# Values of the sampled cross attention: cached rows as weights instead of probabilities as weights

## The reference

```python
def cross_attn(h, mk, mv, wq, wo):
    B, T = h.shape[:2]
    q = (h @ wq).reshape(B, T, CA_HEADS, CA_HD)
    s = jnp.einsum('bthd,bmhd->bhtm', q, mk).astype(jnp.float32) * CA_HD ** -0.5
    p = jax.nn.softmax(s, axis=-1)
    o = jnp.einsum('bhtm,bmhd->bthd', p.astype(mv.dtype), mv).reshape(B, T, CA_HEADS * CA_HD)
    return o @ wo
```

## Time and profile before

| | us |
|---|---|
| median of three runs | 1419.38 |
| the three runs | 1419.38, 1414.24, 1420.62 |
| the profiled execution, its own time | 1415.52 |
| its span, first to last instruction | 1413.7 |
| TensorE busy | 1278.7 (90% of the span) |
| TensorE's weight loads | 1132.2 (80%) |
| VectorE, ScalarE, POOL busy | 538.9, 437.6, 393.7 |

### The profile page before, as it was taken

The page is one execution under the profiler, slowest core; times in us unless marked ns, Lnnn a source line. Parts: engine busy times, 40 slices in busy tenths (PEclk is TensorE's granted clock), DMA queues, the critical chain, the costliest instruction groups (busy, mean ns, idle before and its releaser), DMA issues.

```text
span 1413.7 us, 20837 instructions
## 1 busy us (share of the span) xinstructions
PE 1278.7 (90%) x9132; PEld 1132.2 (80%) x9132; DVE 538.9 (38%) x697; ACT 437.6 (31%) x731; POOL 393.7 (28%) x245
## 2 busy tenths in 40 slices
PE   6996998999889799898968999797999999999995
PEld 5995455777548799787867998496999999999994
DVE  4122143654121325565250034125666666630003
ACT  5224544554331312332132333212222222221111
POOL 1141102000121326122545420032443344433440
PEclk9998998999899899778988999899999999999998
DMA  6332312000341424201444333411122222222211
GB/s 193 121 93 75 112 45 99 22 1 1 105 165 33 124 86 164 75 8 45 154 159 149 120 120 148 180 60 60 60 90 90 90 90 90 90 83 83 83 53 63
DMA packets 91209, 130.14 MB, mean 92 GB/s; under 512 B 6472, under 2 KB 78560, under 8 KB 88816
## 3 DMA queue, kind: packets, MB, share of 16 engines
q1 hardware_dynamic: 83104, 101.61, 22.0%
q0 software_dynamic: 8016, 27.21, 5.7%
HBM read 120.38 MB, written 12.59 MB: 94 GB/s over the span
## 4 chain that ended last, share of the span: by engine, by line
PE 81%; DVE 8%; ACT 5%; DMA 2%; issue 2%; POOL 2%; SPq 0%; DVEq 0%; ACTq 0%; POOLq 0%
PE ring L658 42%; PE ring L632 5%; PE hold L766 5%; PE hold L863 3%; PE ring L1103 2%; PE ring L991 2%; PE ring L834 2%; PE hold L951 2%; POOL weight_lo L563 2%; PE ring L609 2%; PE hold L921 2%; PE ring L642 1%; PE ring L845 1%; PE ring L1185 1%; ACT arena L1437 1%
## 5 line engine op out<-in xcount | busy, mean ns | idle before, releaser
L563 POOL TENSOR_TENSOR weight_lo<-w_ring,weight_hi 128x1024 fp32r<-128x1024 f32 (+1 forms) x124 | 301.0, 2429 | 570.6 <-ACT weight_hi L1324 562.9
L658 PE MATMUL ring<-operand_hi,weight_hi 128*128 128x272 f32 (+1 forms) x1296 | 274.4, 293 | 28.4 <-POOL weight_lo L563 10.3
L658 PE MATMUL ring<-operand_lo,weight_hi 128*128 128x272 f32 (+1 forms) x1296 | 271.6, 291 | 0.0
L658 PE MATMUL ring<-operand_hi,weight_lo 128*128 128x272 f32 (+1 forms) x1296 | 271.4, 291 | 0.0
L1324 ACT ACTIVATE weight_hi<-w_ring 128x1024 fp32r<-128x1024 f32 (+1 forms) x135 | 139.9, 1038 | 369.0 <-PE ring L658 306.2
L658 PEld LDWEIGHTS ring<-operand_hi,weight_hi 128*128 128x128 f32 (+1 forms) x1296 | 206.4, 191 | 33.6 <-issue 23.8
L658 PEld LDWEIGHTS ring<-operand_hi,weight_lo 128*128 128x128 f32 (+1 forms) x1296 | 206.1, 190 | 0.4
L658 PEld LDWEIGHTS ring<-operand_lo,weight_hi 128*128 128x128 f32 (+1 forms) x1296 | 205.8, 190 | 0.4
L1304 ACT ACTIVATE arena<-ring 128x1024 f32<-128x1024 f32 (+10 forms) x113 | 81.2, 725 | 180.3 <-PE ring L658 59.9
L766 PE MATMUL hold<-arena,w_ring 128*128 128x504 f32 (+1 forms) x192 | 81.9, 536 | 12.5 <-ACT arena L1437 7.4
L2233 DVE TENSOR_TENSOR x_res<-x_res,ring 128x544 f32<-128x544 f32 x24 | 17.3, 721 | 186.9 <-PE ring L658 186.6
(11 more groups left out here) (360 smaller groups left out, 1975.6 us busy)
## 6 DMA issues: line engine op xcount, KB each, us to landing
w_ring<-in_w_in SPq DMA_DIRECT2D x13, 1024.0 KB, 5.3
w_ring<-in_ffn_w_gate SPq DMA_DIRECT2D x11, 1024.0 KB
w_ring<-in_ffn_w_up SPq DMA_DIRECT2D x11, 1024.0 KB, 5.3
w_ring<-in_ffn_w_down SPq DMA_DIRECT2D x8, 1024.0 KB, 5.1
arena<-in_cache_mem_k SPq DMA_DIRECT2D x6, 1024.0 KB, 6.9
arena<-in_cache_mem_v SPq DMA_DIRECT2D x6, 1024.0 KB, 10.3
w_ring<-in_w_out SPq DMA_DIRECT2D x4, 1024.0 KB, 5.3
w_ring<-in_ca_wk SPq DMA_DIRECT2D x4, 1024.0 KB, 6.5
```

The source lines that it names most:

```text
L563: self.ops.tensor_tensor(half_of(WL, self.x, kk, cols), w, half_of(WH, self.x, kk, cols).bitcast(F32), ALU.subtract).then_inc(sem("weights ...
L658: last = mm(ps[0:cols, hf * 512:hf * 512 + HALF], half_of((WH, WL)[pw], x, KT, cols)[:, i, :], (xh, xl)[px][:, k, hf * HALF:(hf + 1) * HAL ...
```

## The change

The roles of the operands are swapped. A tile of value rows, 128 tokens x 128 features, becomes the weights, and the four probability columns of one head of one sample are streamed. The result is feature-major, 128 features x 4 tokens, and is written where it belongs in a `ring` item of 128 x 256 (8 feature tiles x 32 sample columns), so that one copy by ScalarE takes it to `MX`. The hold item `cO`, the copy to `crow` and the eight transposes are gone. The samples are taken one by one in the order of the loads, and each signals `cross_values_used` (or `psum_full` for the last), so that SP waits for two signals instead of one. The other sample's columns of `yPT` are not read any more; POOL's memset of them is gone, and with it its wait, and ScalarE waits for the end of the key output (`mem_k_out`) itself, since `yPT` lies over the buffer which that output reads.

```diff
--- before.py
+++ after.py
@@ -286,7 +286,7 @@
     hold = [("h",) + x for x in CGROUPS] + [("o", i, g) for i in range(QT) for g in range(NG)]
     for rd in range(2):
         hold += [("Ss", rd), ("Sw", rd), ("PV", rd)]
-    hold += [("As",)] + [("dSs", h) for h in range(HH)] + [("cS",), ("cO",)]
+    hold += [("As",)] + [("dSs", h) for h in range(HH)] + [("cS",)]
     raws = [("c", kv, n) for kv, g4 in CGROUPS for n in group_tiles(kv, g4)]
     for rd in range(2):
         raws += [(k, rd, b) for k in ("sk", "wk", "sv", "wv") for b in range(4)]
@@ -439,7 +439,6 @@
         KX = take("ca", 2048).rearrange("p (s n) -> p s n", s=2)
         norm_rows = nc.alloc_sbuf_tensor_at("norm_rows", [P, 1024], F32, offset=base["rstd"])[:, :]
         KT4 = [KX[:, 0, :], KX[:, 1, :], mst_all[:, 768:1792], norm_rows]
-        crow = QC.rearrange("p k t -> p (k t)")[:, 0:DM]
 
         def rounded(name, at, n):
 
@@ -1218,25 +1217,17 @@
             cross_probs_t(3)
             cross_weigh(3)
             evac(pe, ("csPT",))
-            open_hold(("cO",))
-
-            for pair in ((0, 2), (4, 6), (1, 3), (5, 7)):
-                for b in pair:
-                    _, s, c = cross_in("v", b)
-                    pe.wait_ge(s, c)
-                for hf in range(2):
+            ps = open_item(("csO",))
+            for b in (0, 2, 4, 6, 1, 3, 5, 7):
+                raw, s, c = cross_in("v", b)
+                pe.wait_ge(s, c)
+                for d in range(KT):
+                    q = 16 * (b % 2) + DS * (d // 2)
+                    at = d * NSMP + DS * b
                     for j in range(2):
-                        for b in pair:
-                            q = 32 * (b // 2)
-                            last = mm(HOLD[q:q + 32, hf * 512:(hf + 1) * 512], yPT[:, j, b, :],
-                                      cross_in("v", b)[0][:, j, hf * 512:(hf + 1) * 512], start=(b % 2 == 0 and j == 0),
-                                      stop=(b % 2 == 1 and j == 1))
-                last.then_inc(hold_full if b == DB - 1 else sem("cross_values_used"), 1)
-            ps = open_item(("csO",))
-            pe.wait_ge(hold_free, hold[("cO",)] + 1)
-            for d in range(KT):
-                last = tr(ps[:, d * P:(d + 1) * P], crow[:, d * P:(d + 1) * P], ident)
-            last.then_inc(psum_full, 1)
+                        last = mm(ps[:, at:at + DS], raw[:, j, d * P:(d + 1) * P], yPT[:, j, b, q:q + DS],
+                                  start=(j == 0), stop=(j == 1))
+                last.then_inc(psum_full if b == DB - 1 else sem("cross_values_used"), 1)
 
             def crossed(k):
                 pe.wait_ge(sem("crossed"), k + 1)
@@ -1666,7 +1657,7 @@
             fn(yP, HOLD[:, 0:MEM], EXP, bias=msc[:, 0:1], scale=CSCALE,
                accum_out=msc[:, 1:2]).then_inc(hold_free, 1)
             weighed_out(2)
-            act.wait_ge(sem("cross_cleared"), 2)
+            act.wait_ge(sem("mem_k_out"), 16)
             key = ("csPT",)
             full(act, key)
             for b2 in range(2):
@@ -1679,17 +1670,8 @@
                     step(ins)
             probs_out(3)
             weighed_out(3)
-            act.wait_ge(hold_full, hold[("cO",)] + 1)
-            fn(crow, HOLD[:, :], COPY).then_inc(hold_free, 1)
             key = ("csO",)
-            full(act, key)
-            for h in range(CH):
-                ins = fn(MX[:, 2 * h:2 * h + 2, SEQ:TOK].rearrange("p k (b t) -> p k b t", b=DB),
-                         slot(key)[:, 2 * h * P:(2 * h + 2) * P].rearrange("p (k b h t) -> p k b h t", k=2, b=DB,
-                                                                          h=CH)[:, :, :, h, :], COPY)
-                if h < CH - 1:
-                    step(ins)
-            ins.then_inc(freed(key), 1)
+            copy_out(key, MX[:, :, SEQ:TOK], slot(key)[:, 0:KT * NSMP].rearrange("p (k n) -> p k n", k=KT))
             evac(act, key)
             act.wait_ge(hold_free, len(hold))
             for i in range(QT):
@@ -2490,10 +2472,6 @@
                     evac(pool, (c, n))
                 g.dma_start(out[name].rearrange("l b (m p) h d -> p (l b m) (h d)", p=P), src).then_inc(
                     sem("mem_k_out" if c == "wk" else "mem_v_out"), 16)
-            lo.upto(splits[("wq", 3, 1)])
-            pool.wait_ge(sem("mem_k_out"), 16)
-            full(pool, ("mkT", 1))
-            g.memset(yPT.rearrange("p j b n -> p (j b n)"), 0.0).then_inc(sem("cross_cleared"), 1)
             lo.upto(splits[("wo", 0, 1)])
             pool.wait_ge(sem("mem_v_out"), 16)
             pool.sem_inc(sem("store_phase"), 1)
@@ -2625,7 +2603,7 @@
             cross(6, 10)
             full(sp, ("cx", 7, 1))
             cross(10, 14)
-            sp.wait_ge(sem("cross_values_used"), 1)
+            sp.wait_ge(sem("cross_values_used"), 2)
             cross(14, 16)
             for c in order[cross_at + 2:]:
                 weights(c)
```

## The result

The changed kernel takes 1450.72 us (median of four runs, 1448.24 to 1451.48), the kernel before 1419.14 us beside it. The ratio is 1.0226, with a 95% interval of 1.0198 to 1.0253: slower by 31.6 us. The forecast was 1449 us, in a range of 1434 to 1457. The profiled execution behind the rows took 1450.21 us.

What follows compares the result with a forecast made beforehand. TensorE was taken to bound the kernel (81% of the chain of waits). Stage +33.8, tail -2.9 and projection start +0.5 sum to +31.4 us, giving 1446.9 or 1450.8 by base; forecast 1449 us, range 1434 to 1457.

Steps and rivals of the forecast that it cites:

- The choice of the low clock: Sampled-value stage: TensorE's clock falls to 0.50 about 3.5 us after the start and stays down until the projection.
- 31- and 4-column stretches: Earlier trace: TensorE busy 3.40 of 3.40 and 3.30 of 3.30 us with few columns, then clock 0.50.
- idle-gap reading: Skill's rule on avoiding idle gaps: a value stage without gaps keeps its clock, so the sum is +8 at most.
- The stage: Sampled-value matmuls: 31 records at 111 ns, 225 at 213 ns, 51.4 us in place of 17.6, +33.8.
- The tail: Between last value matmul and first `operand_hi` copy: one 128x256 copy, 0.4 us in place of 3.3, -2.9.
- The projection's start: Output projection's first records: half clock for 4.5 us loses 2.0 us, against 1.5 before, +0.5.
- forecast's own range: Whole kernel without the rivals: 1441 to 1457 us, from base 1414 to 1421 and +28 to +35.
- Costed at nothing: SP's load queue: last loads, released 10.5 us after stage start, land with 20 us of cover; no TensorE wait.
- The clock stayed at 1.00: Rival for the value stage: TensorE never idles, clock holds; +8.0, or +6.5 without the dip, 1424 to 1425 us; chance 0.08.
- the dip: Before the projection: clock at 0.50 for 3.3 us after the pause, which lost 1.5 us in the kernel before.
- Loads that overlap in one long series of full-width tiles: Rival for the value stage: 128-column loads overlap enough for 57 ns a record, kernel faster at 1410 us; chance 0.03.

Runs made afterwards that it cites:

- the control: The changed kernel still streaming 4 columns, but with another order of results in the PSUM slot and two 128x128 copies instead of one 128x256: 1448.3 us, one run.
- the doubled run: The changed kernel with each of its 128 matmuls of 4 columns issued twice: 1509.0 us, one run.
- the run with 64 columns: The changed kernel with each matmul streaming 64 columns instead of 4, and two 128x128 copies instead of one: 1428.35 us, 1.0058 of the kernel before.

## Why the prediction was right

**The mechanism.** The price is the load of 128 weight columns per record, at the clock of the moment. Run by run: the columns of the weights set it (weights of 32 columns), those streamed do not, up to the 64 that were run, and the lower clock doubles it. The choice of the low clock for nearly the whole stage was the step on which everything hung; the 31- and 4-column stretches of the earlier trace rows spoke for it and the idle-gap reading against.

**The stage.** Forecast 51.4 us and +33.8; measured 49.9 and +32.3. The clock fell 4.8 us after the start and not 3.5, so that 43 records and not 31 had the low price: 12 x 102 ns = 1.2 us. The two prices, 111 and 213 ns, were right within a nanosecond. The 3.5 us came from one stretch; with 4 columns the clock fell 4.8 us after the start here, 5.0 in the control and 3.1 in the doubled run, so that being this near was partly luck.

**The tail.** Forecast -2.9; measured 946.98 to 947.42, 0.4 us in place of 3.3. The copy took 0.384 us, where the line between two sizes had given 0.38.

**The projection's start.** Forecast half clock for 4.5 us; it was 4.0 (949.05 to about 953.1), +0.3 instead of +0.5.

**Sum.** +31.4 forecast, +32.3 - 2.9 + 0.3 = +29.7 by the traces, +31.6 by the medians. The rest of 2 us is not in this stage, and it is the size of the spread of the runs: the profiled execution before was 3.9 us under its median, and the stage, behind code that is all but unchanged, starts between 892.4 and 901.4 us in the eleven traces of this study. The two profiled executions differ by 34.7 us (1450.21 and 1415.52), of which 4.7 lie ahead of the stage. That 31.4 and 31.6 agree to 0.2 us is luck: the stage was put 1.5 us too dear, and the spread made up for it. The ends of the forecast's own range add up to 1442 and 1456, not 1441 and 1457, which changes nothing.

**Costed at nothing.** SP's wait for two samples released the last loads 9.0 us after the start (10.5 forecast), and nobody waited. In the run with 32-column weights, where TensorE is fast enough, the same wait came back on the chain for 8 us. The cover was real, and it was the slow stage itself; it held at full clock too, as the 28.55 us of the run with 64 columns have no wait in them.

**Rivals.** The clock stayed at 1.00 in the run with 64 columns, whose 1428.35 us lie 8.2 over the 1420.12 of the kernel before beside it; that rival had +8.0 with the dip, and the dip stayed. Loads that overlap in one long series of full-width tiles do not exist here: 111 ns held over 512 records. The table of the Trainium skill ("TensorE: Matmul & The Clock Gate", section "Back-to-back issue gap") has some 60 cycles, or a sequencer's 62 ns, for a matmul of up to 64 columns; at 62 ns the stage would be an estimated 16 us. The section gives this for a matmul by itself and says that it leaves out the weight load, so it is no price for this stage: with a new 128-column load each time the runs have 28.6 us at full clock and 49.9 here.

## What to carry to other kernels

For a product with few rows on one side, count the weight columns that must be loaded, since a 128x128 fp32 load costs 111 ns a record at full clock and 213 at half clock, whether 4 columns follow it or 64 (64 at half clock in the earlier trace rows). In this stage the large operand was better on the streaming side, even at the price of transposes: 17.6 us with a wait in it and 9.5 without, each with 3.3 us of tail, against 28.6 at best with full-width loads and 29.6 with strips. Read the granted clock of a stretch that resembles the new stage before costing it: TensorE can be busy all the time and still run at 1.2 GHz, and the wait of 4.1 us for a load cost twice that here, through the clock behind it. And look whether a wait can be bought off with a buffer that is already dead, before the computation is turned round.

## What the runs showed of the hardware that was not expected

Weight loads of 32 columns into four different column strips overlap in full: 14.8 ns each at granted clock 0.50, against 59 ns in one strip, and 8.5 against 33 at 1.00. At that pace something else held TensorE up, most likely the supply of instructions: bursts of 128 records, mostly 1.9 to 2.0 us, then pauses of mostly 1.4 to 2.1 us and one of 4.2 to 4.6, at either clock, so that the stage came to about 29 ns a record (29.6 us for 1024). And surplus streaming can pay: 60 surplus columns a matmul went with a clock that stayed up and took 21.4 us off the stage.
